# Transposed inverse sums instead of scaled probabilities, with a shorter lag, in a hybrid attention encoder step

## Chip, cores and metric

One NeuronCore of a Trainium2 chip. The metric is the device time of one launch in microseconds.

## The reference

The kernel computes one step of a two-layer encoder. Each layer normalises its input, projects it with one matrix, and runs three kinds of attention side by side on parts of the result: FoX (4 heads of 64, causal, with a forget bias), MLA (8 heads from low-rank latents, with a rotary part) and sliding-window attention (4 heads with sinks, called swa). Their outputs are concatenated, projected, and followed by an MLP. There are 1024 prompt tokens (8 tiles of 128) and 8 streams of 16 new tokens (a ninth tile). The part that matters here is the softmax and the product with the values:

```python
p = jax.nn.softmax(jnp.where(mask, logits, NEG_INF), axis=-1)
return jnp.einsum('bhqk,bkhd->bqhd', p.astype(v.dtype), v)
...
sink = jnp.broadcast_to(sinks.reshape(SWA_KV_HEADS, g)[:, :, None, None].astype(jnp.float32),
                        logits.shape[:-1] + (1,))
p = jax.nn.softmax(jnp.concatenate([logits, sink], axis=-1), axis=-1)[..., :-1]
out = jnp.einsum('bnkgqs,bnskd->bnqkgd', p.astype(v.dtype), v)
```

## The kernel before

Each engine has its own instruction stream, written out by hand, and semaphores between them. A layer goes through its input projection, the prompt's attention, the streams' attention, the output projection and the MLP. The change is in the prompt's attention alone.

That stage walks over a list UNITS. For each query tile t it holds `q1` (the MLA query product and the rotary part), the FoX units, `q2` (transposition of the MLA queries, put after the second FoX unit), one swa unit with four heads, and the MLA units. A unit has as many heads as fit two PSUM banks: in tiles 4 to 7 one head for FoX and MLA, in tiles 2 and 3 two, in tile 1 four, in tile 0 four for FoX and eight for MLA. In tile 7 the ninth tile's q1 and q2 stand ahead of the last FoX unit and behind the swa unit.

All engines run the same loop over i, and each does its part of several units in one turn, in program order. A turn's parts before the change:

- TensorE: transposes the probabilities of unit i-3 (LAG_T = 3) in blocks of 128x128 through banks 4 and 5; then the scores of unit i into banks 0/1 or 2/3; then the value products of the group that ended with unit i-4 (LAG = 4) into bank 6 or 7. A group is a unit, or a pair of one-head units.
- VectorE: copies every even chunk (up to four transposed blocks) of unit i-3 to SBUF (L1745); scales the probabilities of unit i-2 (LAG_N = 2): for swa it adds the sink's term to the sums (L1753), takes the reciprocal of the sums (L1754) and multiplies head by head (L1757); then takes the negated maximum of unit i's scores (L1782 for MLA, L1789 for FoX and swa, which also adds the bias), or the six rotary instructions (L1767 to L1772) if the unit is q1.
- ScalarE: copies the odd chunks of unit i-3 (L1317); takes the exponential of unit i with its sum (L1338); copies the value products of the group that ended with i-4 to omixT (L1354).

TensorE waits for the scaling (`norm_ok`) before it transposes a unit. Chunk ch uses bank 4 + ch % 2, so it waits until chunk ch-2 has been copied. The copies go into a ring of 8 buffers ptb. The scores of unit i need the banks of unit i-2, whose exponential (or maximum, for FoX and swa) must be over. GpSimd has little to do in this stage, and the stores of omixT to HBM are issued by SyncE when a tile's last group is copied.

Of the kernel before, what the change touches and what calls it, by code (L numbers as in the profile page):

```python
# [14 lines left out]
ALU = mybir.AluOpType  # L15
# [6 lines left out]
P = 128  # L22
# [53 lines left out]
LAG_T = 3  # L76
LAG = 4
# [46 lines left out]

ATTN, CHUNK0 = {}, {}
_chunks = 0
for _u in range(len(UNITS)):
    if is_attn(_u):
        ATTN[_u] = len(ATTN)
        CHUNK0[_u] = _chunks  # L130
        _chunks += (len(key_blocks(_u)) * UNITS[_u][3] + 3) // 4
# [44 lines left out]
DVE_CHAIN = 8 + 2 * NT + (NATTN + 2 * NSWA) + (2 * NI + 4)  # L176
# [31 lines left out]
def hybrid_step(nc, a, c, o):  # L208

    (y_p, y_s, fk_p, fv_p, lf_p, ckv_p, kr_p, sk_p, sv_p, fk_s, fv_s, lf_s, ckv_s, kr_s, sk_s, sv_s) = o  # L210
    with ExitStack() as ctx:
# [142 lines left out]
        qzf = [at(f"qzf{i}", (RING + 47104, HT + 71296)[i], [P, FOX_H, P]) for i in range(2)]  # L354
        qzs = [at(f"qzs{i}", NRM + 8192 + i * 2048, [P, SWA_H, P]) for i in range(2)]
# [33 lines left out]

        pbuf_b = [bits(f"pbuf{i}", RING + i * 4096 if i < 3 else NRM, [P, NPT * P]) for i in range(4)]  # L390
# [92 lines left out]
        norm_ok = signal("probs_normalised", NATTN)  # L483
# [685 lines left out]
        def _(act):  # L1169
# [8 lines left out]
            for l in range(DEPTH):  # L1178
# [130 lines left out]
                for i in range(len(UNITS) + LAG):  # L1309
                    if i >= LAG_T and i - LAG_T < len(UNITS) and is_attn(i - LAG_T):  # L1310
                        for ch, blocks in chunks_of(i - LAG_T):
                            if ch % 2:
                                act.wait_ge(pt_mm.sem, pt_mm.at(l, ch + 1))
                                if ch >= NPTB:
                                    act.wait_ge(pv_mm.sem, pv_mm.at(l, group_of_chunk(ch - NPTB) + 1))
# [30 lines left out]
                    if i >= LAG and group_ending(i - LAG) is not None:  # L1346
                        n = group_ending(i - LAG)
                        kind, t, h0, _ = UNITS[GROUPS[n][0]]
                        pairs = sum(UNITS[u][3] for u in GROUPS[n]) // 2
                        act.wait_ge(pv_mm.sem, pv_mm.at(l, n + 1))  # L1350
                        if t >= 2 and n == TILE_END[t - 1]:
                            act.wait_ge(mix_out[t % 2].sem, mix_out[t % 2].at(l, 16 * (t // 2)))
                        c0 = {"fox": 0, "mla": 2, "swa": 6}[kind] + h0 // 2
                        nc.scalar.copy(omixT[t % 2][:, c0:c0 + pairs, :].rearrange("p k n -> p (k n)"),  # L1354
                                       bank(6 + n % 2)[:, 0:pairs * P]).then_inc(o_ev.sem, 1)
# [251 lines left out]
        def _(dve):  # L1607
# [15 lines left out]
            for l in range(DEPTH):  # L1623
# [113 lines left out]
                for i in range(len(UNITS) + LAG):  # L1737
                    if i >= LAG_T and i - LAG_T < len(UNITS) and is_attn(i - LAG_T):
                        for ch, blocks in chunks_of(i - LAG_T):
                            if ch % 2 == 0:  # L1740
                                dve.wait_ge(pt_mm.sem, pt_mm.at(l, ch + 1))
                                if ch >= NPTB:
                                    dve.wait_ge(pv_mm.sem, pv_mm.at(l, group_of_chunk(ch - NPTB) + 1))
                                w = len(blocks) * P
                                nc.vector.tensor_copy(ptb[ch % NPTB][:, 0:w], bank(4)[:, 0:w]).then_inc(pt_dve.sem, 1)  # L1745
                    if LAG_N <= i < len(UNITS) + LAG_N and is_attn(i - LAG_N):
                        u = i - LAG_N
                        kind, t, h0, heads = UNITS[u]
                        n, w = ATTN[u], len(key_blocks(u)) * P
                        sums, inv = den[:, n % 4, 0:heads], rinv[:, n % 4, 0:heads]  # L1750
                        dve.wait_ge(sm_done.sem, sm_done.at(l, u + 1))
                        if kind == "swa":
                            chain.link(nc.vector.tensor_tensor(sums, sums, es[:, n % 4, 0:heads], ALU.add))  # L1753
# [956 lines left out]
```

## Time and profile before

| what | value |
|---|---|
| median of the runs | 2833.5 us (2830.48 to 2834.81, 3 runs) |
| the profiled execution | 2821.3 us, its span 2819.4 us |
| granted TensorE clock, mean | 0.99 of full speed |
| TensorE, VectorE, ScalarE busy | 96%, 62%, 37% of the span |
| prompt attention, layer 1 and 2 | 279 and 282 us |

The span runs from the first to the last instruction. Busy shares over the span are means over stages that differ; windows cut out the stage that the change touches.

### The profile page before, as it was taken

What the parts mean: (1) busy time and instruction counts of PE and PEld (TensorE: products, weight loads), DVE (VectorE), ACT (ScalarE), POOL (GpSimd) and SP (SyncE); (2) the same over time, 40 slices, a digit from 0 to 9 for tenths busy, and PEclk for the clock granted to TensorE, in tenths of its full rate; (3) what the DMA queues carried; (4) which work ended last, traced back from release to release, by engine and by line L of the source; (5) the groups of instructions that cost most, each with busy time, mean ns of one, the idle gap of its engine ahead of it and who ended that gap; (6) DMA issues with size and microseconds to landing.
All of it is one profiled execution on the core that took longest, in us unless ns stands there. A gap on an engine that the chain in (4) does not pass through costs nothing.

```text
span 2819.4 us, 39619 instructions
## 1 busy us (share of the span) xinstructions
PE 2697.5 (96%) x14966; PEld 2175.5 (77%) x14966; DVE 1742.5 (62%) x2196; ACT 1054.5 (37%) x1969; POOL 1049.3 (37%) x594
## 2 busy tenths in 40 slices
PE   8998999899999999999999989999999999999997
PEld 6985666787888887888879756667878888878886
DVE  4036777635564559888740467775365464688887
ACT  4225545423423233333332255554243233333333
POOL 1111000114545456767511210001145445567766
PEclk9999999999999999999999999999999999999999
DMA  4212001432343456343132200023423433654441
GB/s 144 64 30 61 25 17 44 136 135 98 123 156 114 151 187 242 127 141 128 62 115 66 65 22 17 17 66 114 164 76 134 153 134 130 251 178 141 134 145 74
DMA packets 164722, 308.75 MB, mean 110 GB/s; under 512 B 24720, under 2 KB 90416, under 8 KB 164592
## 3 DMA queue, kind: packets, MB, share of 16 engines
q1 hardware_dynamic: 161280, 303.59, 31.3%
q10 hardware_dynamic: 3312, 3.41, 0.4%
q8 instruction: 84, 1.38, 0.2%
q14 instruction: 46, 0.38, 0.0%
HBM read 207.40 MB, written 97.72 MB: 108 GB/s over the span
## 4 chain that ended last, share of the span: by engine, by line
PE 83%; DVE 9%; issue 3%; ACT 2%; DMA 2%; POOL 1%; SPq 0%; DVEq 0%; ACTq 0%
PE ps L2574 7%; PE ps L2484 7%; PE ps L2578 7%; PE ps L2576 7%; PE ps L2485 7%; PE ps L2486 7%; PE ps L2250 6%; PE ps L2100 6%; PE ps L2102 6%; PE ps L2101 6%; PE ps L2094 5%; PE ps L2301 3%; PE ps L2217 1%; PE ps L2361 1%; PE ps L2429 1%
## 5 line engine op out<-in xcount | busy, mean ns | idle before, releaser
L2574 PE MATMUL ps<-wq_hi,sa_hi 128*128 128x512 f32 x896 | 349.3, 390 | 5.3 <-DVE x L2030 5.3
L2578 PE MATMUL ps<-wq_hi,sa_lo 128*128 128x512 f32 x896 | 348.7, 389 | 0.0
L2576 PE MATMUL ps<-wq_lo,sa_hi 128*128 128x512 f32 x896 | 348.6, 389 | 0.0
L2030 DVE TENSOR_TENSOR x<-ps,x 128x1024 f32<-128x1024 f32 x224 | 264.2, 1213 | 54.8 <-PE ps L2578 50.5
L1968 DVE TENSOR_TENSOR sa_lo<-ra,sa_hi 128x1024 fp32r<-128x1024 f32 x112 | 279.3, 2495 | 23.4 <-ACT sa_hi L1471 23.4
L1082 POOL TENSOR_TENSOR wq_lo<-wsum,wq_hi 128x1024 fp32r<-128x1024 f32 x64 | 157.4, 2461 | 289.7 <-ACT wq_hi L1451 289.7
L2100 PE MATMUL ps<-w_hi,hT_hi 128*128 128x512 f32 (+2 forms) x672 | 248.4, 370 | 0.2 <-DVE hT_lo L1640 0.2
L2102 PE MATMUL ps<-w_hi,hT_lo 128*128 128x512 f32 (+2 forms) x672 | 246.2, 366 | 0.0
L2101 PE MATMUL ps<-w_lo,hT_hi 128*128 128x512 f32 (+2 forms) x672 | 245.4, 365 | 0.0
L1960 DVE TENSOR_TENSOR cq<-ps,cq 128x1024 f32<-128x1024 f32 x48 | 58.6, 1222 | 285.3 <-ACT cq L1512 243.2
L1088 POOL TENSOR_TENSOR wq_lo<-bsum,wq_hi 128x1024 fp32r<-128x1024 f32 x64 | 171.5, 2690 | 113.3 <-ACT wq_hi L1462 113.3
L2484 PE MATMUL ps<-hT_hi,wq_hi 128*128 128x512 f32 x512 | 203.2, 397 | 7.6 <-DVE hT_lo L1924 7.6
L1088 POOL TENSOR_TENSOR wq_lo<-rq,wq_hi 128x1024 fp32r<-128x1024 f32 x64 | 170.1, 2667 | 93.9 <-ACT wq_hi L1462 93.9
L2486 PE MATMUL ps<-hT_hi,wq_lo 128*128 128x512 f32 x512 | 201.5, 394 | 0.0
L2574 PEld LDWEIGHTS ps<-wq_hi,sa_hi 128*128 128x128 f32 x896 | 168.1, 188 | 43.1 <-issue 7.4
L2485 PE MATMUL ps<-hT_lo,wq_hi 128*128 128x512 f32 x512 | 201.3, 393 | 0.0
L994 POOL TENSOR_TENSOR w_lo<-w_raw,w_hi 128x1024 fp32r<-128x1024 f32 (+2 forms) x32 | 71.2, 2228 | 336.0 <-ACT w_hi L1186 336.0
L2578 PEld LDWEIGHTS ps<-wq_hi,sa_lo 128*128 128x128 f32 x896 | 168.2, 188 | 35.2
L2576 PEld LDWEIGHTS ps<-wq_lo,sa_hi 128*128 128x128 f32 x896 | 168.2, 188 | 34.3
L1082 POOL TENSOR_TENSOR wq_lo<-rq,wq_hi 128x1024 fp32r<-128x1024 f32 x64 | 170.5, 2674 | 57.8 <-ACT wq_hi L1451 57.3
L1512 ACT COPY cq<-ps 128x512 f32<-128x512 f32 x128 | 73.3, 587 | 277.7 <-PE ps L2486 161.3
L2484 PE MATMUL ps<-T_hi,wq_hi 128*128 128x512 f32 x384 | 150.3, 391 | 1.4 <-POOL wq_lo L1082 1.3
(323 smaller groups left out, 6188.7 us busy)
## 6 DMA issues: line engine op xcount, KB each, us to landing
ra<-hidden_scratch SPq DMA_DIRECT2D x112, 512.0 KB, 3.3
hidden_scratch<-cq SPq DMA_DIRECT2D x94, 512.0 KB, 2.7
rq<-in_w_up_dram SPq DMA_DIRECT2D x64, 512.0 KB, 3.9
rq<-in_w_down_dram SPq DMA_DIRECT2D x64, 512.0 KB, 4.3
residual_scratch<-x SPq DMA_DIRECT2D x27, 512.0 KB, 3.1
x<-residual_scratch SPq DMA_DIRECT2D x27, 512.0 KB, 7.9
x<-in_x_prompt_dram SPq DMA_DIRECT2D x16, 512.0 KB, 6.7
w_raw<-in_w_in_dram SPq DMA_DIRECT2D x16, 512.0 KB, 4.5
```

The costliest lines, as they stand in the source:

```text
L1082: nc.gpsimd.tensor_tensor(wq_lo[o % 4][:], up_source(o)[:], wq_hi[o % 4][:], ALU.subtract).then_inc(up_lo.sem, 1)
L1088: nc.gpsimd.tensor_tensor(wq_lo[k][:], down_b_source(o)[:], wq_hi[k][:], ALU.subtract).then_inc(b_lo.sem, 1)
L1968: nc.vector.tensor_tensor(low.rearrange("p k n -> p (k n)"), raws, high.rearrange("p k n -> p (k n)"), ALU.subtract).then_inc(a_lo.sem, 1)
L2100: pe.matmul(out, ah, bh, start=(k == 0), stop=False)
L2101: pe.matmul(out, ah, bl, start=False, stop=False)
L2102: last = pe.matmul(out, al, bh, start=False, stop=(k == n - 1))
L2484: pe.matmul(out, wh[:, cols], h[:, k, :], start=new and k == 0, stop=False, skip_group_check=True)
L2485: pe.matmul(out, wh[:, cols], lo_h[:, k, :], start=False, stop=False, skip_group_check=True)
L2486: last = pe.matmul(out, wl[:, cols], h[:, k, :], start=False, stop=k == 3, skip_group_check=True)
L2574: pe.matmul(out, ah[:, k, :], bh[:, k * 512:(k + 1) * 512], start=new and k == 0, stop=False, skip_group_check=True)
L2576: pe.matmul(out, ah[:, k, :], bl[:, k * 512:(k + 1) * 512], start=False, stop=False, skip_group_check=True)
L2578: last = pe.matmul(out, al[:, k, :], bh[:, k * 512:(k + 1) * 512], start=False, stop=final and k == 1, skip_group_check=True)
```

## The change

The probabilities are no longer scaled. Instead VectorE writes the reciprocal of each query's sum 64 times side by side (tile `ginv`, one column for each output column of the head). TensorE transposes these columns, two heads to one block of 128x128, as the last blocks of the unit's chunks; for one-head units this is done with the odd head. They are copied with the other blocks into ptb. VectorE then multiplies the value products with the copied block (in place of ScalarE's copy) and writes omixT. The transpositions stand two units behind the scores (three before), the value products three (four before). In VectorE's turn the reciprocal now comes first, then the copies of chunks, the maximum, and last the multiplication. A buffer of ptb is free when the multiplication is done, no longer when the value products are. A unit has at most four heads, so the MLA unit of tile 0 becomes two. With the inverse blocks a layer has 170 chunks instead of 144; an odd one-head unit of tile 7 (9 blocks), a two-head unit of tile 3 (9) and the four-head units with two key tiles (10: all of tile 1, and swa in the later tiles) have three chunks.

```diff
-LAG_T = 3
-LAG = 4
+LAG_T = 2
+LAG = 3
+TAIL = 4
...
-    n = min(HEADS[kind], 1024 // head_stride(kind, t))
+    n = min(HEADS[kind], 4, 1024 // head_stride(kind, t))
...
+def inverse_blocks(u):
+    _, _, h0, heads = UNITS[u]
+    return heads // 2 if heads > 1 else h0 % 2
...
+    blocks += [("inverse", k) for k in range(inverse_blocks(u))]
...
+def inverse_place(u):
+    ch, i = divmod(len(key_blocks(u)) * UNITS[u][3], 4)
+    assert i + inverse_blocks(u) <= 4
+    return CHUNK0[u] + ch, i * P
...
+        ginv = at("ginv", LATT + 9216, [P, 4, 4, HD])
...
@@ -1306,13 +1323,13 @@
-                                    act.wait_ge(pv_mm.sem, pv_mm.at(l, group_of_chunk(ch - NPTB) + 1))
+                                    act.wait_ge(o_ev.sem, o_ev.at(l, group_of_chunk(ch - NPTB) + 1))
...
-                    if i >= LAG and group_ending(i - LAG) is not None:
...
-                        nc.scalar.copy(omixT[t % 2][:, c0:c0 + pairs, :].rearrange("p k n -> p (k n)"),
-                                       bank(6 + n % 2)[:, 0:pairs * P]).then_inc(o_ev.sem, 1)
...
@@ -1734,28 +1741,25 @@
-                for i in range(len(UNITS) + LAG):
+                for i in range(len(UNITS) + TAIL):
+                    if LAG_N <= i < len(UNITS) + LAG_N and is_attn(i - LAG_N):
...
+                        dve.wait_ge(sm_done.sem, sm_done.at(l, u + 1))
+                        if kind == "swa":
+                            chain.link(nc.vector.tensor_tensor(sums, sums, es[:, n % 4, 0:heads], ALU.add))
+                        nc.vector.reciprocal(ginv[:, GROUP_OF[u] % 4, g0:g0 + heads, :],
+                                             sums.unsqueeze(2).broadcast_to([P, heads, HD])).then_inc(inv_ok.sem, 1)
                     if i >= LAG_T and i - LAG_T < len(UNITS) and is_attn(i - LAG_T):
...
-                        chain.link(nc.vector.reciprocal(inv, sums))
-                        for g in range(heads):
-                            probs = pbuf[n % 4][:, g * w:(g + 1) * w]
-                            last = nc.vector.tensor_scalar(probs, probs, inv[:, g:g + 1], None, ALU.mult)
-                        last.then_inc(norm_ok.sem, 1)
...
+                    if i >= LAG and group_ending(i - LAG) is not None:
...
+                        ch, i0 = inverse_place(i - LAG)
+                        if ch % 2:
+                            dve.wait_ge(pt_act.sem, pt_act.at(l, ch // 2 + 1))
...
+                        dve.wait_ge(pv_mm.sem, pv_mm.at(l, n + 1))
+                        nc.vector.tensor_tensor(omixT[t % 2][:, c0:c0 + pairs, :].rearrange("p k n -> p (k n)"),
+                                                bank(6 + n % 2)[:, 0:pairs * P],
+                                                ptb[ch % NPTB][:, i0:i0 + pairs * P],
+                                                ALU.mult).then_inc(o_ev.sem, 1)
...
@@ -2268,15 +2286,21 @@
-                    pe.wait_ge(norm_ok.sem, norm_ok.at(l, n + 1))
+                    pe.wait_ge(sm_done.sem, sm_done.at(l, u + 1))
...
+                            if g == "inverse":
+                                if b == 0:
+                                    pe.wait_ge(inv_ok.sem, inv_ok.at(l, n + 1))
+                                src = ginv_b[:, GROUP_OF[u] % 4, 2 * b:2 * b + 2, :].rearrange("p h d -> p (h d)")
...
+                            last = turned(bank(4 + ch % 2)[:, i * P:(i + 1) * P], src)
```

## Rows read from the trace of the kernel before

**Rows 1.** The page, busy time of the whole span: engine, us, share, instructions.

```profile
PE 2697.5 (96%) x14966; PEld 2175.5 (77%) x14966; DVE 1742.5 (62%) x2196; ACT 1054.5 (37%) x1969; POOL 1049.3 (37%) x594
```

**Rows 2.** Windows; after the window and its length: busy us of each engine, clock, DMA.

```profile
236.00:515.00 279.00, 259.58 (x2016) 178.85 (x2016) 205.03 (x516) 147.22 (x404) 9.65 (x24) 0.99 0.10 32
1631.00:1913.00 282.00, 261.87 (x2031) 180.40 (x2029) 205.03 (x516) 148.09 (x408) 10.34 (x25) 0.99 0.10 31
...
252.00:256.00 4.00, 2.02 (x22) 1.60 (x23) 3.96 (x20) 0.09 (x1) 0.95 (x2) 1.00 0.01 2
256.00:260.00 4.00, 4.00 (x17) 2.85 (x16) 1.80 (x6) 3.62 (x11) 0.00 (x0) 0.57 0.00 0
```

**Rows 3.** The waits, window 236 to 515: who waited for whom, us, times, longest.

```profile
PE ps L2094 <- DVE pbuf L1757: 12.7, 18, 2.5
...
PE ps L2094 <- ACT ptb L1317: 2.1, 3, 0.7
...
PE ps L2301 <- ACT ptb L1317: 0.6, 1, 0.6
```

**Rows 4.** Windows of line L1757 alone, the scaling of the probabilities.

```profile
236.00:515.00 279.00, 56.27 (x128) 0.99 0.10 32
```

**Rows 5.** VectorE's instructions by form, 236 to 515: busy us, mean ns, idle before.

```profile
L1745 DVE COPY ptb<-ps 128x512 f32<-128x512 f32 x72 | 49.4, 687 | 20.0 <-PE ps L2094 19.9
...
L1782 DVE TENSOR_REDUCE negm<-ps 128x1 f32<-128x1024 f32 x8 | 9.8, 1222 | 4.1 <-PE ps L2250 4.1
...
L1754 DVE RECIPROCAL rinv<-den 128x1 f32<-128x1 f32 x48 | 7.4, 154 | 0.0
...
L1782 DVE TENSOR_REDUCE negm<-ps 128x1 f32<-128x640 f32 x8 | 6.6, 820 | 0.1
...
L1767 DVE TENSOR_TENSOR ropet<-qtok,cs 128x128 f32<-128x128 f32 x9 | 2.6, 292 | 20.6 <-ACT qtok L1323 20.6
...
L1754 DVE RECIPROCAL rinv<-den 128x4 f32<-128x4 f32 x12 | 2.1, 177 | 3.5 <-ACT pbuf L1338 3.3
...
L1754 DVE RECIPROCAL rinv<-den 128x2 f32<-128x2 f32 x12 | 1.9, 156 | 0.0
...
L1754 DVE RECIPROCAL rinv<-den 128x8 f32<-128x8 f32 x1 | 0.2, 196 | 0.0
```

**Rows 6.** Timeline in tile 7, two MLA heads: start, us, engine, line, tiles, count.

```profile
494.11 1.97 PE L2301 MATMUL ps<-ptb,Vm 128*64 128x128 f32 x32
494.22 1.23 DVE L1782 TENSOR_REDUCE negm<-ps 128x1 f32<-128x1024 f32 x1 [0.18 <-PE ps L2250]
495.48 1.12 ACT L1338 ACTIVATE pbuf<-ps,negm 128x1024 f32<-128x1024 f32 x1 [1.18 <-DVE negm L1782]
...
496.01 0.88 PE L2094 MATMUL ps<-identR,pbuf_bits 128*128 128x128 f32 x8
...
496.72 1.95 PE L2250 MATMUL ps<-kTm,qTm 104*128 104x512 f32 x4
496.92 0.58 ACT L1317 COPY ptb<-ps 128x512 f32<-128x512 f32 x1
```

**Rows 7.** Timeline in tile 6, TensorE: products, blocks, scores.

```profile
430.69 1.75 PE L2301 MATMUL ps<-ptb,Vf 128*64 128x128 f32 x28
432.37 0.79 PE L2094 MATMUL ps<-identR,pbuf_bits 128*128 128x128 f32 x7
433.00 1.74 PE L2250 MATMUL ps<-kTm,qTm 104*128 104x512 f32 x4
```

**Rows 8.** Timeline, a tile's first query product and the last rotary instruction.

```profile
448.52 2.81 PE L2217 MATMUL ps<-wuq,latT 128*128 128x384 f32 x8
...
453.47 0.28 DVE L1772 TENSOR_TENSOR qtok<-qtok,ropet 128x128 f32<-128x128 f32 x1
```

**Rows 9.** Timeline in tile 6, the window unit's maxima.

```profile
421.33 0.48 DVE L1789 CUSTOM_DVE_ANT_0 pbuf<-ps,bias,nsink 128x256 f32<-128x256 f32 x1
...
423.07 0.16 DVE L1797 TENSOR_TENSOR es<-negm,nsink 128x4 f32<-128x4 f32 x1
```

More of the change, by code:

```diff
@@ L482, in hybrid_step @@
         pt_act = signal("probsT_copied_act", NCHUNK // 2)
-        norm_ok = signal("probs_normalised", NATTN)
+        inv_ok = signal("sums_inverted", NATTN)
         pv_mm = signal("values_product", len(GROUPS))
@@ L1734, in _ @@
                                                    ALU.add))
-                for i in range(len(UNITS) + LAG):
+                for i in range(len(UNITS) + TAIL):
+                    if LAG_N <= i < len(UNITS) + LAG_N and is_attn(i - LAG_N):
+                        u = i - LAG_N
+                        kind, t, h0, heads = UNITS[u]
+                        n, g0 = ATTN[u], h0 % 2 if heads == 1 else 0
+                        sums = den[:, n % 4, 0:heads]
+                        dve.wait_ge(sm_done.sem, sm_done.at(l, u + 1))
[3 more added lines that the diff above has]
+                                             sums.unsqueeze(2).broadcast_to([P, heads, HD])).then_inc(inv_ok.sem, 1)
                     if i >= LAG_T and i - LAG_T < len(UNITS) and is_attn(i - LAG_T):
@@ L1798, in _ @@
                                                             ALU.subtract).then_inc(max_done.sem, 1)
+                    if i >= LAG and group_ending(i - LAG) is not None:
+                        n = group_ending(i - LAG)
+                        kind, t, h0, _ = UNITS[GROUPS[n][0]]
+                        pairs = sum(UNITS[u][3] for u in GROUPS[n]) // 2
+                        ch, i0 = inverse_place(i - LAG)
+                        if ch % 2:
+                            dve.wait_ge(pt_act.sem, pt_act.at(l, ch // 2 + 1))
+                        if t >= 2 and n == TILE_END[t - 1]:
+                            dve.wait_ge(mix_out[t % 2].sem, mix_out[t % 2].at(l, 16 * (t // 2)))
+                        c0 = {"fox": 0, "mla": 2, "swa": 6}[kind] + h0 // 2
+                        dve.wait_ge(pv_mm.sem, pv_mm.at(l, n + 1))
[3 more added lines that the diff above has]
+                                                ALU.mult).then_inc(o_ev.sem, 1)
                 nc.vector.tensor_copy(qpeS[0:ROPE].rearrange("p s h q -> p h s q"),
@@ L2277, in probs_transposes @@
                         for i, (g, b) in enumerate(blocks):
-                            c0 = (g * len(tiles) + b - tiles[0]) * P
-                            last = turned(bank(4 + ch % 2)[:, i * P:(i + 1) * P], pbuf_b[n % 4][:, c0:c0 + P])
+                            if g == "inverse":
+                                if b == 0:
+                                    pe.wait_ge(inv_ok.sem, inv_ok.at(l, n + 1))
+                                src = ginv_b[:, GROUP_OF[u] % 4, 2 * b:2 * b + 2, :].rearrange("p h d -> p (h d)")
+                            else:
+                                c0 = (g * len(tiles) + b - tiles[0]) * P
+                                src = pbuf_b[n % 4][:, c0:c0 + P]
+                            last = turned(bank(4 + ch % 2)[:, i * P:(i + 1) * P], src)
                         last.then_inc(pt_mm.sem, 1)
@@ L2305, in values @@
                     last.then_inc(pv_mm.sem, 1)
-                for i in range(len(UNITS) + LAG):
+                for i in range(len(UNITS) + TAIL):
                     if i >= LAG_T and i - LAG_T < len(UNITS) and is_attn(i - LAG_T):
```

22 lines of the change are left out of this document (4 added, 18 removed).

## Prediction

> **What bounds the kernel now.** I read the page's busy shares first, then the attention stage by windows, then its waits, then the order of instructions in it. Over the whole span TensorE is busy 96% and VectorE 62% [rows 1]. The change touches one stage, which runs once per layer: 279 us of the first layer and 282 us of the second [rows 2]. There TensorE is busy 259.6 us and idle 19.4 us; VectorE is busy 205.0 us, so it is the second engine by far, and the two layers agree within 2 us. The idle time of TensorE is what a better order could win. The wait table says who ends it: 12.7 us per layer end with VectorE's scaling of the probabilities (L1757), and 2.1 us with a copy of transposed blocks by ScalarE [rows 3]. So about 15 us per layer, 30 in all, is the most that removing these waits can bring; the rest is filling, draining and rotary work that stays.
>
> **What it removes and adds in busy time, per layer.** VectorE loses 128 scalings, 56.3 us [rows 4], and the narrow reciprocals, 7.4 + 1.9 + 2.1 + 0.2 = 11.6 us [rows 5]. It gains 50 multiplications that take the place of ScalarE's copies of the value products, and 74 reciprocals that write each sum's inverse 64 times, since a head's inverse must be a block of 64 columns to be transposed. The trace has no reciprocal wider than 8. From 4 to 8 columns it grows from 177 to 196 ns, 4.75 ns a column, where a reduction over 1024 columns takes 1222 ns, 1.2 ns a column [rows 5]: a reciprocal is slower per column than other work. I take 4.75 because it is the step nearest to the wide end: 196 + 56 x 4.75 = 0.46 us for one head, 0.77 for two, 1.37 for four. The bounds are 1.2 ns (0.23, 0.31, 0.46 us) and the step from 2 to 4 columns, 10.5 ns (0.78, 1.45, 2.80 us). Units of one, two and four heads number 48, 12 and 14: 22.1 + 9.2 + 19.2 = 50.5 us. A multiplication of 128 columns is taken as the rotary one, 0.29 us [rows 5], one of 256 as 0.42 (0.13 more for 128 columns at about 1 ns): 36 and 14 of them, 16.3 us. So VectorE changes by -67.9 + 66.8 = -1 us: it is not relieved at all. ScalarE stays far from bounding.
> **A**: TensorE gains 64 inverse transpositions (128 head-and-tile inverses, two to a block of 128 columns). Eight transpositions take 0.71 us from 496.01 to 496.72 [rows 6], 0.089 each: **+5.7 us**.
>
> **What moves.** Per iteration i TensorE issues transpositions, scores of unit i, value products. Before, the transpositions were those of unit i-3 and waited for a scaling that VectorE had issued an iteration earlier, ahead of the maximum of i-1. Now they are those of i-2. The probabilities themselves need only ScalarE, which is early enough. But the inverse block, the last of the unit, needs the reciprocal, and VectorE's queue puts that behind the maximum of unit i-1 and behind the new multiplication of iteration i-1, which waits for value products that TensorE issued just before. Behind the inverse block on TensorE wait the scores of unit i, and with them everything. A chain appears that goes once around in nearly every iteration: scores, maximum, multiplication, reciprocal, inverse block, scores.
> I walk it for tile 7, with time 0 where scores end and products start (494.11). The products take until 1.90 and the eight blocks until 2.61; the maximum starts 0.11 late and ends at 1.34 [rows 6]. The multiplication can start when the products are done, at 2.0, and ends at 2.3; the reciprocal ends at 2.7. Here the odd head has nine blocks, so three chunks, and the third shares a PSUM bank with the first, which must be copied out: by VectorE after the reciprocal (0.69 us [rows 5], so 3.36), or by ScalarE after its exponential (about 1.2 us from 1.38, then 0.58 [rows 6], so 3.2). TensorE was done at 2.61: it stands 0.7 us. In tile 6 (products 1.68, blocks 0.63 [rows 7]; two chunks) the inverse is there at 1.79 + 0.29 + 0.42 + 0.06 = 2.56 against 2.31: 0.25 us. With fewer keys the cover shrinks faster than the maximum: 0.34 in tile 5, 0.4 in tile 4. The same walk for the other places, per layer:
> **B**, odd heads 3 and 5 of MLA in tiles 4 to 7, 2 x (0.4 + 0.34 + 0.25 + 0.7) = 3.4, and head 1, whose cover is the shorter window product, 0.5 + 0.45 + 0.4 + 1.2 = 2.6: 6.0.
> **C**, the last unit of a tile, behind the next tile's rotary work. The query product ends at 451.33, the rotary ends at 453.75 [rows 8]: 2.42, then multiplication, reciprocal and signal, 3.2 against a cover of 1.7 to 2.3 in tiles 4 to 6 (3.6 in all), and 2.1, 2.2, 2.8, 3.4 in tiles 3 to 0, with their wider reciprocals: 14.1.
> **D**, the fourth FoX head, which comes right behind the scores of the window unit. That unit's maxima run from 421.33 to 423.23, 1.9 us [rows 9], with only 0.5 to 0.7 us of blocks as cover; the inverse is there at 0.1 + 1.9 + 0.46 + 0.06 = 2.5: 2.0 + 1.9 + 1.85 + 2.35 = 8.1; the FoX units with more cover 1.6: 9.7.
> **E**, the window unit itself: four heads, three chunks, reciprocal 1.37 after the next maximum. In tile 6, from the end of its own scores: D lets the next scores end only near 4.2, their maximum ends at 5.4, the sink's term and the reciprocal at 7.0, a copy behind it at 7.6; TensorE has done the eight blocks at 5.0, so 2.3. About 2.1 in tiles 4 to 7 and 1.55 before: 14.5.
> **F**, units of two and four heads, where every unit has inverse blocks: in tile 3 the round is 0.11 + 1.23 + 0.29 + 0.77 + copy 0.6 + 0.16, then scores 1.88 (5.0 to 5.3) where TensorE alone needs 1.02 + 0.72 + 1.88 = 3.62, so 1.5 x 4; in tile 2, with a maximum of 0.95, 3.65 against 2.8, 0.85 x 4; tiles 1 and 0 3.4: 12.8.
> B to F are 57.1 us, A is 5.7, and the waits that go are 12.7 + 2.1 = 14.8, about 15.4 with the few before value products: 57.1 + 5.7 - 15.4 = 47.4 us per layer, **+95 us** in two. The profiled execution took 2821.3 us; the sum gives 2916. The runs' median is 12.2 us above it, so by the median 2833.5 + 95 = **2928 us**. One iteration less lag shortens the drain by what its bubble gave, under 1 us: nothing. ScalarE's load changes by 13.8 us of copies gone and some 10 us of larger block copies, and lies under TensorE. The split of tile 0's MLA unit adds one maximum; it is in C and F. The stores of omixT wait for the same signal, from another engine, and nothing waits for them: nothing.
>
> **The price of the reciprocal.** With 1.2 ns a column 23 one-head, 10 two-head and 12 four-head places shrink by 0.23, 0.46 and 0.91 us: 21 us per layer less, +53, 2886 us. With 10.5 ns they grow by 0.32, 0.68 and 1.43: 31 us more, +157, 2991 us. A case between is eight columns' time of ordinary work for each (the reduction's step from 640 to 1024 columns is 1.05 ns a column [rows 5]; 8 x 1.05 = 8.4): 0.67, 1.20, 2.27 us, 20 us more per layer, +135, 2968 us. The Trainium skill speaks for this one: "VectorE: DVE Perf Modes", section "First, the fixed hardware budget", says that a reciprocal is an iterated division with a repeat count of 8. The trace's steps, 4.75 and 10.5 ns, lie on both sides of it, so no row here settles it.
>
> **The rivals.** (1) Reciprocal at full speed: 2886 us. Against it: 177 to 196 ns over four columns. (2) Reciprocal at 8.4 ns: 2968 us. (3) The bubbles cover for each other: a wait at one place lets VectorE and ScalarE get ahead at the next, and half of the 57 us remain: 28.5 + 5.7 - 15.4 = 18.8 per layer, +38, 2871 us. For it: most places lie next to each other around the window unit. Against it: the chain is serial, and being ahead elsewhere doesn't shorten it. (4) The clock: the stretch 252 to 256, in which TensorE was busy only 2.02 of 4 us, was followed by one at 0.57 of the clock, 1.7 us lost [rows 2]. Were each of the seven other window units per layer to cause one more, 14 x 1.7 = 24 us on top: 2952. (5) The other side: the inverse is always early. In tile 6 the multiplication ends at 2.08 and the blocks at 2.31, so it needs a reciprocal with its signal under 0.23 us, and at the window unit a maximum that doesn't stand before it; then only 5.7 - 15.4 = -9.7 per layer remains, -19, 2814 us, faster. For it: VectorE idles in the stage for 74 us per layer. Against it: the queue's order. (6) Gain and loss cancel, within 0.2% (5.7 us, about what a measurement of this kernel can tell from none).
>
> **How the numbers follow.** Forecast 0.39 (its own range 2900 to 2950), (1) 0.12, (2) 0.13, (3) 0.13, (4) 0.13, (5) 0.07, (6) 0.03. Slower is all but the last two: 0.90; same 0.03; faster 0.07. The range goes from below (3) to between (2) and the upper bound of the reciprocal: 2860 to 2985. It leaves out (5), (6) and that bound, some 1.5 in 10.
>
> **What would show it.** In the profile after, the reciprocal's rows of 64, 128 and 256 columns give the price directly: 0.46, 0.77, 1.37. The wait table must show TensorE's transpositions waiting for the reciprocal (the inverse) and, in tiles 3 and 7, for copies of blocks, some 55 us per layer; the stage must last about 327 us with 265 us of TensorE. VectorE's busy time there stays near 204. I am wrong if TensorE's idle time in the stage is under 20 us, or if most of it ends with ScalarE's exponential, which I take to be early, or if lower clock levels explain the growth.

## The result, and the profile after

The change made the kernel slower: 3010.4 us (3000.9 to 3014.0, 4 runs) against 2834.2 us (2830.5 to 2837.4, 4 runs), a ratio of 1.0632 with a 95% interval of 1.0595 to 1.067. The forecast was 2928 us, with a range up to 2985. The direction was right and the size half of what came: +176 us by the medians. The profiled executions differ by 186.4 us (spans of 2819.4 and 3005.8 us; that of the kernel before lies some 12 us under its median), and all that follows is read from them.

The page after the change, its span, busy times and the two rows that show TensorE and its clock in 40 slices:

```profile
span 3005.8 us, 39829 instructions
...
PE 2784.8 (93%) x15094; PEld 2230.1 (74%) x15094; DVE 1760.2 (59%) x2070; ACT 1059.7 (35%) x1897; POOL 1047.6 (35%) x594
...
PE   8997788899999999999999977888999999999997
...
PEclk9997899999999999999999978899999999999999
```

TensorE's busy share falls from 96% to 93% [rows 1], but its busy time rises by 87.3 us (2784.8 less 2697.5). Its idle time rises by the rest of 186.4, 99.1 us. The change adds only 64 small transpositions per layer to TensorE, 5.7 us by the prediction. So about 76 of the 87.3 us are the same work taking longer. The two dents in the rows are the attention of each layer.

The windows of layer 1's prompt attention (tiles 0 to 3, tiles 4 to 7, the whole stage from the first query product on; columns as in [rows 2]):

```profile
234.20:383.50 149.30, 108.87 (x627) 73.04 (x628) 79.47 (x175) 54.37 (x167) 6.33 (x16) 0.81 0.03 12
383.50:610.80 227.30, 197.11 (x1467) 134.49 (x1467) 133.32 (x278) 95.96 (x204) 3.69 (x9) 0.93 0.11 32
234.00:610.80 376.80, 305.98 (x2093) 207.56 (x2093) 212.99 (x453) 150.39 (x371) 10.02 (x25) 0.88 0.08 24
```

The same two parts before:

```profile
234.20:322.50 88.30, 79.52 (x572) 54.91 (x572) 63.56 (x205) 52.08 (x171) 6.49 (x16) 0.98 0.05 20
322.50:515.90 193.40, 182.76 (x1459) 125.81 (x1457) 141.70 (x313) 95.13 (x234) 3.16 (x8) 0.99 0.12 36
```

The stage went from 281.7 to 376.6 us: +94.9. TensorE's busy time rose from 262.3 to 306.0 us, its idle time from 19.4 to 70.6. Tiles 0 to 3 grew by 61.0 us and tiles 4 to 7 by 33.9. The mean clock says why busy time grew: 0.88 over 376.8 us. TensorE's clock has two levels, 2.4 and 1.2 GHz, so that is 2 x 0.12 x 376.8 = 90 us at the lower one; the stretches of it in the trace sum to 88.7 us, against 6.8 before (one from 256 to 260 [rows 2], one from 512 to 516). Some 58 of them lie in tiles 0 to 3. Layer 2 shows the same: 376.7 us, 69.5 of them idle and 88.7 at the lower clock.

Who ended TensorE's waits in the stage after, answering to [rows 3]:

```profile
PE ps L2112 <- DVE ginv L1753: 33.8, 27, 3.5
PE ps L2112 <- DVE ptb L1762: 18.3, 13, 2.7
PE ps L2112 <- ACT pbuf L1355: 8.5, 7, 1.8
PE ps L2112 <- ACT ptb L1334: 7.9, 10, 2.0
```

L2112 is the transposition, L1753 the wide reciprocal, L1762 and L1334 the copies of blocks by VectorE and ScalarE, L1355 the exponential. The waits for the scaling are gone, as they must be. Those that took their place are four to five times as long: 68.5 us in these four rows, against 15.4.

VectorE's forms after, from 236 to 603 (columns as in [rows 5]; the last few instructions of the stage lie behind):

```profile
L1753 DVE RECIPROCAL ginv<-den 128x64 f32<-128x64 f32 x47 | 25.5, 543 | 0.0
L1753 DVE RECIPROCAL ginv<-den 128x256 f32<-128x256 f32 x14 | 24.5, 1750 | 3.2 <-ACT pbuf L1355 3.0
...
L1753 DVE RECIPROCAL ginv<-den 128x128 f32<-128x128 f32 x12 | 11.3, 943 | 0.0
L1814 DVE TENSOR_TENSOR omixT<-ps,ptb 128x128 f32<-128x128 f32 x34 | 9.8, 289 | 12.3 <-PE ps L2325 12.1
```

The multiplications cost what was taken, 0.29 us (and 0.42 for 256 columns). The reciprocals cost 0.54, 0.94 and 1.75 us where 0.46, 0.77 and 1.37 were taken. VectorE is busy 213 us in the stage, 8 more than before, where the prediction had it near 204.

The timeline of tile 1 after shows both halves of the loss in one piece (start, duration, line, tiles, count; in brackets the idle time before it and what ended it):

```profile
256.35 0.47 PE L2112 MATMUL ps<-identR,ginv_bits 128*128 128x128 f32 x2 [2.07 <-DVE ginv L1753]
256.62 4.24 PE L2235 MATMUL ps<-wuq,latT 128*128 128x384 f32 x8
...
265.42 0.34 PE L2112 MATMUL ps<-identR,ginv_bits 128*128 128x128 f32 x2 [3.51 <-DVE ginv L1753]
```

and VectorE in the same stretch:

```profile
262.99 0.29 DVE L1776 TENSOR_TENSOR qtok<-qtok,ropet 128x128 f32<-128x128 f32 x1
263.20 0.42 DVE L1814 TENSOR_TENSOR omixT<-ps,ptb 128x256 f32<-128x256 f32 x1
263.53 1.74 DVE L1753 RECIPROCAL ginv<-den 128x256 f32<-128x256 f32 x1
```

TensorE stands 3.51 us in front of an inverse block. VectorE comes to the reciprocal only after the rotary work and the multiplication, then spends 1.74 us on it. That is the prediction's place C. The query product at 256.62, behind the previous wait, takes 4.24 us, where the same eight products took 2.81 before [rows 8]: it ran at the lower clock.

### The profile page after: what moved, and what is told of

It reads as the page before. It is cut to its first block, busy times and chain, and to the rows that moved or that the text cites. A ratio compares the mean times of both kernels' runs of the same rounds, so it can differ in the third digit from the quotient of the medians.

```text
span 3005.8 us, 39829 instructions
## 1 busy us (share of the span) xinstructions
PE 2784.8 (93%) x15094; PEld 2230.1 (74%) x15094; DVE 1760.2 (59%) x2070; ACT 1059.7 (35%) x1897; POOL 1047.6 (35%) x594
## 4 chain that ended last, share of the span: by engine, by line
PE 80%; DVE 10%; issue 4%; ACT 3%; POOL 1%; DMA 1%; DVEq 0%; SPq 0%; ACTq 0%; POOLq 0%
PE ps L2268 9%; PE ps L2598 7%; PE ps L2602 7%; PE ps L2600 7%; PE ps L2508 6%; PE ps L2509 6%; PE ps L2510 6%; PE ps L2118 5%; PE ps L2120 5%; PE ps L2119 5%; PE ps L2112 4%; PE ps L2325 3%; DVE ginv L1753 2%; PE ps L2235 2%; PE ps L2385 1%
## 5 line engine op out<-in xcount | busy, mean ns | idle before, releaser
L1099 POOL TENSOR_TENSOR wq_lo<-wsum,wq_hi 128x1024 fp32r<-128x1024 f32 x64 | 157.3, 2459 | 289.7 <-ACT wq_hi L1458 289.7
L2268 PE MATMUL ps<-kTm,qTm 104*128 104x512 f32 (+3 forms) x384 | 177.3, 598 | 0.0
```

Of the source, the lines that this page charges most:

```text
L1099: nc.gpsimd.tensor_tensor(wq_lo[o % 4][:], up_source(o)[:], wq_hi[o % 4][:], ALU.subtract).then_inc(up_lo.sem, 1)
L2268: last = pe.matmul(out[:, c0:c1], q, keys[:, k0 + c0:k0 + c1], start=True, stop=not masked)
```

## The experiments

Two theories stood first. **A**: a chain through VectorE's queue (maximum, multiplication, wide reciprocal, inverse block) sets the pace, and the clock only follows from the waits. **B**: the price is that of the new work itself (wide reciprocals, third chunks, multiplications on VectorE), whatever the lag. All kernels were run beside the kernel before, and the ratio is to the runs of it on the same chip. The table gives, for layer 1, the stage from the first query product to the first product of the streams' attention, TensorE's busy and idle time in it, and the time at the lower clock ("half clock"). In layer 2 the idle time is within 1.4 us of this in every kernel, but the half clock can differ (109.2 and 160.4 us in e2, 27.3 and 41.0 in e11), so only large differences in that column mean something.

| kernel | us | ratio (95%) | stage | busy | idle | half clock |
|---|---|---|---|---|---|---|
| before | 2834.2 | 1 | 281.7 | 262.3 | 19.4 | 6.8 |
| after | 3010.4 | 1.0632 (1.0595–1.067) | 376.6 | 306.0 | 70.6 | 88.7 |
| e1_lag_3_4 | 2954.1 | 1.0439 (1.0414–1.0465) | 342.7 | 291.7 | 51.0 | 63.2 |
| e2_old_scheme_lag_2_3 | 3115.2 | 1.1015 (1.0986–1.1043) | 416.9 | 308.4 | 108.5 | 109.2 |
| e3_narrow_reciprocal | 2949.7 | 1.0427 (1.0401–1.0454) | 348.4 | 298.6 | 49.8 | 71.7 |
| e4_filled_waits | 2971.8 | 1.0507 (1.0481–1.0532) | 357.9 | 318.2 | 39.7 | 10.2 |
| e14_half_filling | 2983.2 | 1.0549 (1.0521–1.0578) | 366.1 | 318.7 | 47.4 | 58.0 |
| e5_lag_3_4_copies_first | 2931.3 | 1.0356 (1.0295–1.0417) | 334.3 | 289.7 | 44.6 | 54.6 |
| e6_lag_3_4_copies_first_narrow | 2907.9 | 1.0275 (1.0217–1.0333) | 321.4 | 282.8 | 38.6 | 37.5 |
| e9_third_chunk_later | 2929.1 | 1.0346 (1.0288–1.0404) | 335.9 | 289.3 | 46.6 | 51.2 |
| e10_reciprocal_before_product | 2987.3 | 1.0548 (1.0489–1.0608) | 367.5 | 303.5 | 64.0 | 95.6 |
| e12_lag_3_4_all_three | 2835.9 | 1.0025 (1.0008–1.0042) | 284.9 | 269.6 | 15.3 | 10.2 |
| e13_lag_2_3_narrow_third | 2890.4 | 1.0207 (1.0173–1.0241) | 318.7 | 283.4 | 35.3 | 37.5 |
| e11_lag_2_3_early_narrow_third | 2882.9 | 1.0192 (1.0157–1.0226) | 309.4 | 276.9 | 32.5 | 27.3 |

Leaving out the two kernels that fill waits, the order by idle time is nearly the order by half clock, and the one kernel whose idle time is down at the level of before (e12) has a half clock near that of before.

### The new scheme at the old lag

```diff
-LAG_T = 2
-LAG = 3
+LAG_T = 3
+LAG = 4
```

> The changed kernel with the lags of before (transpositions three units, values four behind the scores); the wide reciprocals, the inverse blocks and the multiplications stay. Theory A (the short lag puts the inverse behind the next maximum and the multiplication, TensorE waits, and the waits bring its clock down): with a lag of three the reciprocal is issued an iteration before the block is needed, so nearly all of the 176 us go: 2820 to 2870 us, fewer than 6 half-clock stretches per layer, idle time of TensorE in the attention stage under 25 us. Theory B (the price is that of the new work itself: wide reciprocals, third chunks, multiplications on VectorE, whatever the lag): 2930 us or more.

Theory A missed here: the time came down by only 1.9% of the time before, not to the level of before, and lies in theory B's branch. The waits of this kernel in the stage:

```profile
PE ps L2112 <- DVE ptb L1762: 28.2, 14, 5.7
PE ps L2112 <- ACT ptb L1334: 18.5, 15, 3.1
...
PE ps L2112 <- DVE ginv L1753: 0.9, 1, 0.9
```

The waits for the inverse itself fell from 33.8 to 0.9 us, but those for copies of blocks rose from 26.2 to 46.7. The timeline shows how, with an MLA unit of tile 1 behind tile 2's query product:

```profile
280.21 1.09 PE L2112 MATMUL ps<-identR,pbuf_bits 128*128 128x128 f32 x8
...
283.01 1.75 DVE L1753 RECIPROCAL ginv<-den 128x256 f32<-128x256 f32 x1
284.67 0.63 DVE L1762 COPY ptb<-ps 128x512 f32<-128x512 f32 x1
285.36 0.36 PE L2112 MATMUL ps<-identR,ginv_bits 128*128 128x128 f32 x2 [4.05 <-DVE ptb L1762]
```

The inverse is there, but it belongs to a third chunk, which needs the first chunk's bank. The copy that frees the bank now stands behind the rotary work and the reciprocal of another unit. So the scheme has a second cost that this lag doesn't remove: the third chunk and the place of the copy that it waits for.

### The old scheme at the short lag

The kernel before with the new lags, the loops' ends adjusted, and the scaling moved ahead of the copies in VectorE's turn, as the reciprocal is after the change:

```diff
-LAG_T = 3
-LAG = 4
+LAG_T = 2
+LAG = 3
+TAIL = 4
```

> The kernel before with the lags of the change (two and three); the probabilities are scaled as before, the scaling moved ahead of the copies in VectorE's turn because it must come before them. Theory A: every unit's transposition now waits for a scaling that stands behind the next maximum, also for even heads, whose turn has no value products ahead: waits longer and more frequent than in the changed kernel, 3020 to 3200 us. Theory B: the old scheme has none of the new work, so 2834 us within 30.

3115 us, 10.2% over before and slower than the change itself: here theory A's branch is the one that came. The waits:

```profile
PE ps L2095 <- DVE pbuf L1750: 106.5, 67, 4.3
```

Nearly every unit waits for its scaled probabilities before its first block, 67 times per layer, where the new scheme mostly waits in front of its last blocks. In the old scheme the shorter lag (with the scaling moved ahead of the copies, which it needs) thus costs more than the whole change does, and the new scheme softens it. Neither theory is the whole: the lag costs without the new work, and the new work costs without the lag.

### A narrow reciprocal, then a copy of 64 columns

```diff
-                        nc.vector.reciprocal(ginv[:, GROUP_OF[u] % 4, g0:g0 + heads, :],
-                                             sums.unsqueeze(2).broadcast_to([P, heads, HD])).then_inc(inv_ok.sem, 1)
+                        inv = rinv[:, n % 4, 0:heads]
+                        chain.link(nc.vector.reciprocal(inv, sums))
+                        nc.vector.tensor_copy(ginv[:, GROUP_OF[u] % 4, g0:g0 + heads, :],
+                                              inv.unsqueeze(2).broadcast_to([P, heads, HD])).then_inc(inv_ok.sem, 1)
```

> The changed kernel, but the reciprocal is taken of the sums alone (1 to 4 columns) and then copied 64 times side by side on VectorE. If the price of the wide reciprocal (0.54, 0.94 and 1.75 us) is a main term of the chain: about 0.40, 0.45 and 0.6 us in its place, some 20 us less waiting per layer and part of the half-clock time: 2930 to 2975 us. If it is hidden or only the place in the queue matters: 2995 to 3015 us.

As expected, it helped: 2949.7 us, ratio 1.0427, two points of the 6.3 less than the change. The pair of instructions takes the place of 543, 943 and 1750 ns:

```profile
L1755 DVE COPY ginv<-rinv 128x64 f32<-128x64 f32 x48 | 9.4, 195 | 1.7
L1754 DVE RECIPROCAL rinv<-den 128x1 f32<-128x1 f32 x48 | 7.4, 153 | 0.1
L1755 DVE COPY ginv<-rinv 128x256 f32<-128x256 f32 x14 | 4.1, 294 | 0.5
...
L1754 DVE RECIPROCAL rinv<-den 128x4 f32<-128x4 f32 x14 | 2.4, 175 | 2.8 <-ACT pbuf L1355 2.6
```

0.35 us for one head and 0.47 for four. The waits for the inverse fell from 33.8 to 18.6 us, those for VectorE's copies from 18.3 to 11.0: idle time 20.8 us less, and TensorE's busy time, in which nothing was changed, 7.4 us less.

### Filling the waits

This kernel computes everything as the change does and adds, ahead of every wait for an inverse block (or for the bank of a chunk that holds nothing else), four products whose result nobody reads, at 50 places per layer (the trace records each as two instructions, so 400):

```diff
+                def fill(u):
+                    for _ in range(FILL):
+                        pe.matmul(bank(2 * (u % 2))[:, 0:P], identF[:], identF[:], start=True, stop=True)
...
+                        if blocks[0][0] == "inverse":
+                            fill(u)
...
+                                    if i > 0:
+                                        fill(u)
                                     pe.wait_ge(inv_ok.sem, inv_ok.at(l, n + 1))
```

> The changed kernel, with four products of the identity with itself (128x128, fp32, about 0.85 us together, output not used) on TensorE ahead of each wait for an inverse block, written to a score bank that is free. If the half clock costs time of its own (89 us per layer at half, up to 44 us of TensorE's work): the clock stays up, the filling lies in waits that are there anyway, 2930 to 2985 us, although TensorE does 54 us more work per layer. If the half clock costs nothing because TensorE would wait for VectorE anyway: 3010 to 3100 us.

It does more work and is faster, by 1.25% of the time before. Windows of the whole stage, then of the filling products alone:

```profile
234.90:592.80 357.90, 318.17 (x2493) 234.43 (x2493) 212.39 (x453) 150.23 (x370) 10.03 (x25) 0.99 0.08 26
...
234.90:592.80 357.90, 57.17 (x400) 49.22 (x400) 0.99 0.08 26
```

The clock is 0.99 again and half clock 10.2 us. The work that took 306.0 us in the change takes less: with the filling's 57.2 us taken off, 261.0 us are left. The spans of filling and real work overlap, though, and the real work's own spans in the trace cover 275.0 us. So the clock gave back between 31 and 45 us per layer; half of the 78.5 us less at half clock is 39. The stage became only 19 us shorter, because the filling itself takes time beyond the waits. So the lower clock is caused by the waits and is not an independent loss.

With two products instead of four:

```diff
-FILL = 4
+FILL = 2
```

> As e4 with two products in place of four ahead of each wait for an inverse block, some 27 us of extra work per layer in place of 54. The chain's waits at full clock are in e4 hidden among the filling; less filling shows them better. If the clock still stays up: 2930 to 2970 us, under e4, and the clock's own price in the changed kernel is then the larger part of the difference to it. If the clock falls again with half the filling: 2975 to 3010 us, with more than 40 us at half clock per layer.

2983.2 us, and half clock 58.0 us: half the filling did not keep the level, as the second branch said. It gives 0.8 points against 1.25 for four.

### At the old lag: copies first, then the narrow reciprocal too

Copies of chunks ahead of the reciprocal in VectorE's turn, on top of the old lag:

```diff
+                    if i >= LAG_T and i - LAG_T < len(UNITS) and is_attn(i - LAG_T):
+                        for ch, blocks in chunks_of(i - LAG_T):
...
                     if LAG_N <= i < len(UNITS) + LAG_N and is_attn(i - LAG_N):
...
-                    if i >= LAG_T and i - LAG_T < len(UNITS) and is_attn(i - LAG_T):
-                        for ch, blocks in chunks_of(i - LAG_T):
```

> As e1 (lags three and four), and in VectorE's turn the copies of chunks stand ahead of the wide reciprocal again, as before the change. In e1 TensorE waited for copies, not for the reciprocal. If these were late because the reciprocal of the next unit stood ahead of them: most of e1's 120 us over before go, 2840 to 2885 us, and what is left are the units with three chunks (22 per layer at some 0.5 us) and 11 us of transpositions. If the third chunk itself is what e1 waited for, wherever the copy stands: 2920 us or more.

The result is the weak branch: ratio 1.0356 against 1.0439, and with both intervals (0.6 and 0.25 points to a side) only just a gain. Waits for VectorE's copies fell from 28.2 to 17.7 us, those for ScalarE's rose from 18.5 to 21.1.

And the narrow reciprocal on top of it:

```diff
-                        nc.vector.reciprocal(ginv[:, GROUP_OF[u] % 4, g0:g0 + heads, :],
...
+                        chain.link(nc.vector.reciprocal(inv, sums))
+                        nc.vector.tensor_copy(ginv[:, GROUP_OF[u] % 4, g0:g0 + heads, :],
```

> As e5, with the narrow reciprocal and a copy of it 64 times side by side (as e3). With the copies first the reciprocal's price should hardly matter, as it is off the chain: within 15 us of e5, 2830 to 2880 us. If the reciprocal's price still counts: 20 us or more below e5.

2907.9 against 2931.3 us on the same chip. The price of the reciprocal still counts, with 0.8 points, at a lag at which TensorE never waits for an inverse. What still stands in the way is seen in tile 7:

```profile
526.91 1.23 DVE L1788 TENSOR_REDUCE negm<-ps 128x1 f32<-128x1024 f32 x1 [1.14 <-PE ps L2270]
528.05 0.68 DVE L1752 COPY ptb<-ps 128x512 f32<-128x512 f32 x1
...
528.79 0.28 PE L2114 MATMUL ps<-identR,ginv_bits 128*128 128x128 f32 x1 [1.27 <-DVE ptb L1752]
```

The first chunk's copy, although first in its own turn, comes behind the previous turn's maximum, which itself came late, and the ninth block waits for it.

### The third chunk behind the scores

On TensorE, chunks beyond the second are transposed after scores(i) instead of before; the lag is the change's 2 and 3:

```diff
-                    for ch, blocks in chunks_of(u):
+                    for ch, blocks in chunks_of(u)[2:] if third else chunks_of(u)[:2]:
...
                     if i < len(UNITS):
                         scores(i)
+                    if i >= LAG_T and i - LAG_T < len(UNITS) and is_attn(i - LAG_T):
+                        probs_transposes(i - LAG_T, third=True)
```

> The changed kernel (lags two and three), but a unit's third chunk is transposed behind the scores of that turn, not ahead of them. It takes away the wait for the copy of the first chunk (26 us of TensorE's 71 us idle per layer in the changed kernel's attention stage) and, in those 22 units, the wait for the inverse ahead of the scores: 2900 to 2960 us. If the third chunk is only a small term beside the reciprocal's place: 2985 us or more.

2929.1 us: 2.9 points less than the change. Its waits:

```profile
PE ps L2112 <- DVE ginv L1753: 27.2, 24, 3.5
...
PE ps L2112 <- ACT ptb L1334: 4.7, 6, 1.5
...
PE ps L2112 <- DVE ptb L1762: 3.0, 6, 1.0
```

The waits for copies fell from 26.2 to 7.7 us; those for the inverse went only from 33.8 to 27.2.

### The reciprocal earlier in the turn

LAG_N = 1 and the reciprocal's block between the maximum and the multiplication, so that it no longer waits for the value products (the block itself is unchanged and moved down):

```diff
-LAG_N = 2
+LAG_N = 1
```

> The changed kernel (lags two and three), but the wide reciprocal is taken one turn earlier, between the maximum and the multiplication, so that the inverse block waits for neither the next maximum nor the multiplication; the copies come first in the turn. Theory A, by the place in the queue: the 34 us per layer of waiting for the reciprocal go nearly all, with part of the half clock, and copies come earlier too: 2880 to 2940 us. If it is the price of the reciprocal, or ScalarE's exponential, that holds the chain wherever the reciprocal stands: 2970 us or more.

2987.3 us, ratio 1.0548: 0.8 points less, at the edge of what the intervals tell apart, and in the weak branch: the multiplication is not what holds the reciprocal. The waits for the inverse only went from 33.8 to 27.6 us. The expectation misread its own edit in one point. A unit's reciprocal now stands right behind the next unit's maximum, in the same turn; in the change it stands behind that maximum too, at the head of the following turn. So the edit takes only the multiplication out of the way, and the wait for the next maximum stays. A kernel with the reciprocal ahead of that maximum was not run.

### All three cures together, at either lag

The old lag with copies first, the narrow reciprocal and the third chunk behind the scores; the edits are those shown above:

```diff
-LAG_T = 2
-LAG = 3
+LAG_T = 3
+LAG = 4
...
+                        chain.link(nc.vector.reciprocal(inv, sums))
...
+                        probs_transposes(i - LAG_T, third=True)
```

> Lags three and four, copies first, narrow reciprocal with a copy (as e6), and the third chunk behind the scores (as e9). If the third chunk's wait is what is left in e6 (34 us of TensorE's idle time per layer, and with it 37 us at half clock): the idle time of the stage falls to 10 us or less and the time to 2810 to 2840 us, level with the kernel before or a little under it (11 us of transpositions more, some 25 us of waits for the scaling less). If another wait takes its place: 2860 us or more.

2835.9 us (12 runs) against 2827.3 (17 runs), ratio 1.0025 (1.0008 to 1.0042): the time is in the range expected and the loss is all but gone, though the idle time fell to 15.3 us and not to 10. The stage, a piece of what follows it, and the whole streams' attention behind it:

```profile
232.70:517.60 284.90, 269.57 (x2093) 189.06 (x2093) 179.29 (x525) 147.88 (x370) 9.71 (x24) 0.98 0.10 31
522.00:530.00 8.00, 8.00 (x32) 6.27 (x30) 3.84 (x10) 2.36 (x8) 2.20 (x9) 0.50 0.81 236
517.60:587.80 70.20, 66.19 (x506) 56.31 (x504) 36.70 (x106) 27.38 (x71) 9.81 (x13) 0.90 0.32 107
```

and that last one in the kernel before:

```profile
515.90:581.10 65.20, 60.30 (x508) 51.78 (x505) 35.09 (x103) 27.81 (x73) 9.75 (x13) 1.00 0.34 115
```

The stage lasts 284.9 us, 3.2 more than before, with VectorE 26 us less busy (179.3 against 205.3). TensorE's 269.6 us are 7.3 more than before; 1.7 of these are half of the 3.4 us more at half clock (10.2 against 6.8), and the other 5.6 are the inverse blocks, the 5.7 of the prediction's A. The idle time is 4.1 us less. Most of what is left of the loss lies behind the stage: the streams' attention takes 70.2 us against 65.2, with the clock at 0.90 against 1.00 and the same work in it. That is 5 us per layer. Why the clock falls there was not tried.

The narrow reciprocal and the third chunk behind the scores at the change's lag:

```diff
+                        chain.link(nc.vector.reciprocal(inv, sums))
...
+                        probs_transposes(i - LAG_T, third=True)
```

> The changed kernel's lags and order (two and three), with the narrow reciprocal and the third chunk behind the scores. Alone they gave about 58 and 81 us back. If terms add: 2865 to 2885 us. What is left over e12 is the price of the short lag itself: ScalarE's exponential and the place behind maximum and multiplication, 30 to 60 us. If they overlap (one wait behind the other): 2900 us or more.

And with the reciprocal earlier in the turn as well, by LAG_N = 1 and the moved block:

> As e13, and the reciprocal between the maximum and the multiplication of the turn before, copies first (as e10). If the place in the queue is what e13 still pays: 15 to 40 us below e13, 2835 to 2865 us. If e13 pays for the exponential and for copies behind the maximum: within 15 us of e13 or above it.

2890.4 and 2882.9 us, ratios 1.0207 and 1.0192. The first lies between its two branches; the second is within 15 us of the first, so having the multiplication out of the reciprocal's way is worth nothing that can be told here either. Against the old lag's 1.0025 on the same chip, the short lag is still worth 1.8 points (51 us). The copies' place differs there as well; but the second kernel has the copies first, as the kernel at the old lag has, and is still 1.7 points above it. The waits left are for the inverse (16.0 and 13.4 us) and for the exponential (10.0 and 12.0).

## Why the prediction was right in direction and wrong in size

**The account.** By spans the change cost 186 us where the sum gave 95. Split by TensorE: busy time was to grow by 11.4 us and grew by 87.3; idle time was to grow by 2 x 41.7 = 83.4 and grew by 99.1. So of the 91 us that were missing, 76 are busy time and 16 idle time.

**The step that failed** is the clock: the sum puts it at nothing and has it only as rival (4). The prediction read the one stretch at 0.57 behind a busy share of half [rows 2], and took it as a price of 1.7 us for each of 14 window units, 24 us, with a chance of 0.13. In place of one stretch for each window unit there came 88.7 us of half clock per layer instead of 6.8: 82 us more, which costs about half of that in busy time, and 38 us were measured (43.7 more, less 5.7 for the inverse blocks). The place was wrong too. Two thirds of it lies in tiles 0 to 3, where C and F put many of their waits: TensorE stood 2.1 to 3.5 us at every unit of tiles 0 and 1 and up to 2.9 in tiles 2 and 3, and its next products often ran at the lower level. The filled kernel shows the cause: with the waits filled, half clock goes from 88.7 to 10.2 us. With half of the 82 us put on the sum for each layer, 2928 + 82 = 3010, which is the median that came (by the spans 177 of the 186 us). That uses the measured half clock; no row of the kernel before gave its size, and what the rows did give was the sign, one stretch at the lower level behind a half-idle one. The prediction had named it as a sign of being wrong: lower clock levels do explain 76 of the 186 us.

**The waits (B to F)** came where the walk put them. Summed over each unit's inverse blocks in layer 1, TensorE stood 57.4 us there, against 57.1 in the sum:

| place | sum | measured |
|---|---|---|
| B, MLA heads 1, 3 and 5, tiles 4 to 7 | 6.0 | 5.2 |
| C, last unit of a tile | 14.1 | 13.6 |
| D, FoX units, tiles 4 to 7 | 9.7 | 8.3 |
| E, window units | 14.5 | 13.2 |
| F, other units of two and four heads | 12.8 | 17.1 |

That the total fits so well is in part luck. The wider reciprocal alone should have added 8.1 us: 0.08, 0.17 and 0.38 us more than taken, at the 23, 10 and 12 places that the prediction counted, is 1.8 + 1.7 + 4.6. So other terms of the walk were too large by about as much. (Its one-head walks for B take 0.4 to 0.42 us, not the 0.46 of its own estimate.) F is short in tiles 0 and 1 (6.9 us for 3.4). What the sum lacked are waits ahead of a unit's first block, 11.4 us per layer, which it put at nothing; 8.5 of them end with **the exponential**, which it took to be early, six times in tiles 0 to 3 and once in tile 7. The 11.4 us are about what was missing in the idle time, which grew by 51.2 us per layer where the sum has 41.7.

After the change, tiles 6 and 7:

```profile
505.90 0.28 PE L2112 MATMUL ps<-identR,ginv_bits 128*128 128x128 f32 x1 [2.10 <-DVE ginv L1753]
...
511.34 0.37 PE L2112 MATMUL ps<-identR,ginv_bits 128*128 128x128 f32 x2 [2.69 <-DVE ptb L1762]
511.54 2.79 PE L2268 MATMUL ps<-kTm,qTm 104*128 104x512 f32 x4
...
591.74 0.28 PE L2112 MATMUL ps<-identR,ginv_bits 128*128 128x128 f32 x1 [0.33 <-ACT ptb L1334]
...
599.61 0.28 PE L2112 MATMUL ps<-identR,ginv_bits 128*128 128x128 f32 x1 [0.67 <-DVE ptb L1762]
```

D gave 1.85 in tile 6 and 2.10 was there; E gave 2.3 for 2.69; B gave 0.7 in tile 7 for 0.33 and 0.67. The line at 511.54 is the part that the walk didn't have: the scores behind the wait take 2.79 us, where the same four took 1.74 [rows 7].

**The price of the reciprocal** came out at 6.3 ns a column (from 543 to 943 ns over 64 columns, to 1750 over 128 more), between the 4.75 taken and the 8.4 of rival (2). In the prediction's sum the difference is the 8.1 us per layer just worked out, 16 in all. Making it narrow gave back 2.0 points, 58 us: it takes away nearly the whole reciprocal and not only the part mis-sized, and the half clock fell with the waits, from 88.7 to 71.7 us. Rival (2) would have had 0.67, 1.20 and 2.27 us, 23 to 30% more than the trace shows. The Trainium skill's "VectorE: DVE Perf Modes", section "First, the fixed hardware budget", with its repeat count of 8, spoke for that rival. Rival (1), with 0.23, 0.31 and 0.46 us, is further off.

**A**, the inverse transpositions, is right: about 5.6 us for 5.7, read from e12, whose waits and clock are near those of before.

**Rival (3)**, bubbles that cover for each other, did not come: idle time grew by more than the sum. **Rival (5)** needed the inverse in time, and it is late 27 times per layer.

**What the change is.** Four costs, three of which were undone by themselves: the shorter lag (1.9 points when undone alone, 1.8 with the other cures made), the wide reciprocal (2.0), the third chunk ahead of the scores (2.9), and the clock that follows from their waits (at least 1.25, from the kernel that only fills; the figures before it hold their own share of the clock). They overlap: the sum of the first three alone is over the whole, and the narrow reciprocal with the third chunk gives 4.3 at the change's lag. The last 1.8 points are mostly the lag, since 1.7 are left with the copies first in both; which instruction ahead of the reciprocal holds it was not separated, as the next unit's maximum stands there in every kernel that was run at the short lag. No version tried was faster than the kernel before.

## What to carry to other kernels

Add up the idle time that an edit will give TensorE and then ask for its clock: over the kernels here that fill nothing and wait more than before, each microsecond idle above the 19 of before went with 1.1 to 2.2 us more at half clock, and in the change that added three quarters to what the waits themselves cost (38 us to 51). When a lag is shortened, walk the queue of the engine that feeds the waiting instruction, including instructions of other units that stand in it, and ask of every added block which buffer it shares and when that is emptied. When an instruction is moved to get it out of another's way, check which instructions still stand ahead of it in the new place. Write an inverse narrow and spread it with a copy; don't compute it 64 times.

## What the runs showed of the hardware

A VectorE reciprocal in f32 costs 6.3 ns a column, six times the 1.05 of a reduction, so 256 columns take 1750 ns; four columns take 175 and the copy that spreads them to 256 takes 294 to 307.

TensorE's clock level does not go with how busy the engine is at the moment. Five windows after, at the end of tile 0 and the start of tile 1:

```profile
248.00:252.00 4.00, 1.86 (x14) 1.12 (x12) 3.27 (x6) 3.13 (x17) 0.00 (x0) 0.84 0.00 0
252.00:256.00 4.00, 2.25 (x14) 2.09 (x14) 2.58 (x3) 1.79 (x9) 0.00 (x0) 0.58 0.00 0
256.00:260.00 4.00, 3.65 (x8) 2.25 (x9) 0.75 (x2) 0.46 (x2) 0.00 (x0) 0.56 0.02 4
260.00:264.00 4.00, 1.91 (x15) 1.00 (x13) 2.20 (x8) 0.80 (x1) 0.00 (x0) 1.00 0.00 0
264.00:268.00 4.00, 2.58 (x11) 1.74 (x11) 1.82 (x2) 0.37 (x1) 0.00 (x0) 0.79 0.00 0
```

Full clock is granted from 260 to 264, in which the engine is busy 1.91 of 4 us, and 0.56 of it from 256 to 260, in which it is busy 3.65. What the engine did just before fits better: ahead of the window at 0.56 it was busy 1.86 and 2.25 of 4 us, and ahead of the one at full clock 3.65. No wait in this stage is longer than 3.51 us, and yet 88.7 of 376.6 us ran at the lower level. And work of no use, four products of 128 columns ahead of each wait for an inverse, made the kernel faster.
